# RMS norm cut into chunks and spread over groups of matmuls, conditioning pieces moved into the first attention, convolution statistics in two banks

## The reference

```python
for l in range(DEPTH):                                   # 4 layers: attention, convolution, attention, convolution
    sh1, sc1, g1, sh2, sc2, g2 = adaln(cond, w_ada[l], b_ada[l])      # silu(cond) @ w + b, six vectors of 1024
    h = modulate(rms_norm(x, norm_g[l, 0]), sh1, sc1)    # x*rsqrt(mean(x*x)+eps)*g, then h*(1+scale)+shift
    if l % 2 == 0:  y = attention(h) @ w_o               # also returns k and v of the context tokens
    else:           y = conv_module(h)                   # below
    x = x + g1 * y
    h = modulate(rms_norm(x, norm_g[l, 1]), sh2, sc2)
    x = x + g2 * (square(relu(h @ w_up[l])) @ w_down[l])
y = rms_norm(x, final_g)

def conv_module(h, ...):
    a, g = split(h @ w_pw1, 2);  u = a * sigmoid(g)
    u = depthwise_conv(u, width 31) + b_dw
    return silu(layer_norm(u, ln_g, ln_b)) @ w_pw2
```

## Time and profile before

| | us |
|---|---|
| median of three runs (lowest, highest) | 3113.19 (3110.22, 3113.33) |
| profiled execution | 3116.69 |
| its span on the slowest core (core 0) | 3115.1 |
| spans of the eight cores | 3084.0 to 3115.1 |
| TensorE, VectorE, ScalarE, GpSimd busy | 2656.1, 1152.1, 1135.2, 303.5 |
| 16 DMA engines, mean traffic | 65 GB/s |

### The profile page before, as it was taken

The page is one execution under the profiler, slowest core; times in us unless marked ns, Lnnn a source line. Parts: engine busy times, 40 slices in busy tenths (PEclk is TensorE's granted clock), DMA queues, the critical chain, the costliest instruction groups (busy, mean ns, idle before and its releaser), DMA issues.

```text
span 3115.1 us, 45413 instructions; the slowest of 8 cores (3084.0 to 3115.1 us)
## 1 busy us (share of the span) xinstructions
PE 2656.1 (85%) x15672; PEld 1154.0 (37%) x15672; DVE 1152.1 (37%) x1707; ACT 1135.2 (36%) x1800; POOL 303.5 (10%) x280
## 2 busy tenths in 40 slices
PE   1976878899997866999989778789999787699995
PEld 0432222344443432444434222234444343244442
DVE  0224453442323435423233444334232334542323
ACT  2424556530305245402153455654020523550214
POOL 0100000000002431000000000000000233200000
PEclk9985555999998998999999655589999898799997
DMA  8774110166652211466436411015665131033322
GB/s 175 122 181 61 8 8 1 28 90 100 102 93 44 56 26 17 79 100 101 78 57 162 90 12 8 1 28 82 95 95 82 29 75 26 1 54 55 54 42 81
DMA packets 107599, 202.28 MB, mean 65 GB/s; under 512 B 41904, under 2 KB 52144, under 8 KB 107376
## 3 DMA queue, kind: packets, MB, share of 16 engines
q0 software_dynamic: 76592, 154.23, 33.1%
q1 hardware_dynamic: 30784, 45.14, 4.4%
HBM read 315.02 MB, written 31.46 MB: 111 GB/s over the span
## 4 chain that ended last, share of the span: by engine, by line
PE 70%; ACT 13%; issue 7%; DVE 5%; DMA 3%; another core or an unknown queue 1%; ACTq 0%; DVEq 0%; SPq 0%
PE ps L612 45%; PE ps L1246 5%; ACT hTs L576 4%; PE ps L1211 3%; PE ps L857 3%; ACT scr L943 2%; PE ps L818 2%; PE ps L1376 2%; PE ps L860 2%; PE ps L636 2%; ACT scr L890 2%; DVE scr L936 1%; PE ps L909 1%; DMA vo<-scr 1%; PE ps L464 1%
## 5 line engine op out<-in xcount | busy, mean ns | idle before, releaser
L612 PE MATMUL ps<-hTs,ring 128*128 128x512 bf16 x3840 | 846.4, 382 | 39.3 <-ACT hTs L576 36.0
L612 PE MATMUL ps<-big,ring 128*128 128x512 bf16 x3072 | 666.7, 379 | 0.0
L612 PEld LDWEIGHTS ps<-hTs,ring 128*128 128x128 bf16 x3840 | 375.4, 98 | 497.4 <-issue 58.7
L677 ACT ACTIVATE big<-ps 128x512 f32<-128x512 f32 x384 | 227.2, 597 | 749.5 <-PE ps L612 741.6
L612 PEld LDWEIGHTS ps<-big,ring 128*128 128x128 bf16 x3072 | 299.2, 98 | 358.5
L679 DVE TENSOR_TENSOR big<-big 128x512 bf16<-128x512 f32 x384 | 265.1, 692 | 388.0 <-ACT big L677 385.5
L654 DVE SCALAR_TENSOR_TENSOR xTs<-ps,mod,xTs 128x512 f32<-128x512 f32 x240 | 178.5, 750 | 532.1 <-PE ps L612 500.6
L396 POOL DMA_DIRECT2D ring<-wall x140 | 100.2, 716 | 2080.7 <-PE ps L612 1385.6
L936 DVE TENSOR_TENSOR scr<-ps,scr 128x512 f32<-128x512 f32 (+7 forms) x384 | 189.9, 531 | 185.6 <-PE ps L922 146.2
L530 ACT ACTIVATE scr<-xTs 128x4096 bf16<-128x4096 f32 x27 | 97.6, 3616 | 435.1 <-DVE xTs L654 354.0
L943 ACT ACTIVATE scr<-scr 128x512 bf16<-128x512 f32 (+7 forms) x384 | 177.0, 503 | 184.6 <-DVE scr L936 152.5
(11 more groups left out here) (88 smaller groups left out, 1957.5 us busy)
## 6 DMA issues: line engine op xcount, KB each, us to landing
ring<-wall POOLq DMA_DIRECT2D x140, 1024.0 KB, 11.2
kTo<-scr SPq DMA_DIRECT2D x48, 256.0 KB, 6.7
vo<-scr SPq DMA_DIRECT2D x48, 256.0 KB, 3.2
scr<-big SPq DMA_DIRECT2D x128, 54.0 KB, 3.4
xTs<-xT SPq DMA_DIRECT2D x3, 2048.0 KB, 53.0
...
```

The costliest lines, as they stand in the source:

```text
L612: ins = e.matmul(ps[pi][:, :], lhsT=w[:, kc, fc * fw:(fc + 1) * fw], rhs=src[:, kc, t * 512:(t + 1) * 512], start=(kc == 0), stop=(kc == n ...
L677: P.op("act", lambda e: e.activation(out=ta[:, :], in_=ps[pi][:, :], func=AF.Relu), reads=[ps_r[pi]], writes=[ta_r])
```

## The change

**Norm.** `norm_begin` now comes before the stage that produces `xT`, and holds three PSUM banks, one per tile, out of `next_ps` (`held`). Behind each residual addition `norm_chunk` squares that one chunk (512 columns) on ScalarE and defers, with a lag of 1, a single sum matmul into the tile's bank. With the eighth the tile's Ln and Exp are issued and its eight outputs (`norm_out`) go on a second list, `bq`. `tick(rate)` first serves `pend`, then takes `rate` entries from `bq`: one as a rule, three in the "down" product. `ensure_h(t)` empties the lists as far as a product needs tile t. `hT_r` is one resource per tile and chunk. This holds for the output products, the second half of "down" in all layers (with the final norm) and "pw2".

**Conditioning.** The first four pieces run ahead of the first norm, the other eight of layer 0 one after each pair of heads in attention. The second and third tile of `xT` are loaded only when the third weight piece has landed.

**Convolution.** The sums of all three tiles of a chunk are six matmuls with a 32-column matrix of ones, each into 32 partitions of one of two banks (6 and 7), so that six banks are free for the rest. Mean and reciprocal deviation are computed once for 96 partitions and spread to 128 by float32 matmuls with `sel`. All tap matrices are built by VectorE, eight during each of "pw1" pieces 1 to 3 and the last eight between chunks. "pw2" writes its input in token order, so that its residual addition needs no strided view, and tile 1's and 2's LayerNorm chunks stand on `bq`.

```diff
-            sem_x[t], writes=[xT_r[c][t] for c in range(8)])
+            sem_x[t], writes=[xT_r[c][t] for c in range(8)],
+            extra=[(ring_sem[2], 16)] if t > 0 else [])
...
     pend = []
-
-    def tick():
+    bq = []
+
+    def tick(rate=1):
         for it in pend:
             it[0] -= 1
         while pend and pend[0][0] <= 0:
             pend.pop(0)[1]()
+        for _ in range(rate):
+            if bq:
+                bq.pop(0)[1]()
...
+    def ensure_h(t):
+        while any(it[1] == t for it in ntiles):
+            if pend:
+                pend.pop(0)[1]()
+            else:
+                bq.pop(0)[1]()
...
+    def norm_chunk(ctx, c, t, lag=1):
+        bk = ctx["bk"][t]
+        sq, sq_r = ctx["sq"][ctx["q"] % 6]
+        ctx["q"] += 1
+        P.op("act", lambda e: e.activation(out=sq[:, :], in_=xT[:, c, t * 512:(t + 1) * 512],
                                            func=AF.Square),
-             reads=[xT_r[c][t] for c in range(8)], writes=[ctx["sqb_r"][t % 2]])
...
+        def part():
+            n = ctx["cnt"][t]
+            ctx["cnt"][t] += 1
+            P.op("pe", lambda e: e.matmul(ps[bk][:, :], lhsT=ones_b[:, :], rhs=sq[:, :],
+                                          start=(n == 0), stop=(n == 7)),
+                 reads=[sq_r, const_r], writes=[ps_r[bk]])
+            if n == 7:
+                norm_rstd(ctx, t)
+                for cc in range(8):
+                    bq.append((t, lambda cc=cc: norm_out(ctx, cc, t)))
+        defer(lag, part)
+
+    def norm_rstd(ctx, t):
+        bk = ctx["bk"][t]
+        rstd, rstd_r = ctx["rstd"][t % 2]
+        P.op("act", lambda e: e.activation(out=rstd[:, :], in_=ps[bk][:, :], func=AF.Ln,
                                            bias=V("epsr"), scale=1.0 / D),
-             reads=[ps_r[pi], vecs_r], writes=[rstd_r])
...
+        P.op("act", lambda e: e.activation(out=ps[bk][:, :], in_=rstd[:, :], func=AF.Exp, scale=-0.5),
+             reads=[rstd_r], writes=[ps_r[bk]])
+
+    def norm_out(ctx, c, t):
         tsl = slice(t * 512, (t + 1) * 512)
-        for c in range(8):
-            ta, ta_r = ctx["tmp"][ctx["n"] % 2]
-            P.op("dve", lambda e, c=c, ta=ta: e.tensor_tensor(
-                out=ta[:, :], in0=xT[:, c, tsl], in1=rps[:, :], op=ALU.mult),
-                reads=[xT_r[c][t], rps_r], writes=[ta_r])
...
                 for fc in range(fc_per_piece):
-                    pi = next_ps(0, pshi)
...
                     evac(j, fc, t, pi)
-                    tick()
-                if last_tile_done is not None and j == npieces - 1:
-                    last_tile_done(t)
+                    tick(rate)
...
+    def resid_evac(gate_chunk0, nctx=None, lag=1):
         def evac(j, fc, t, pi, per_piece=4):
             fch = j * per_piece + fc
             s = slot_of(t)
@@ -656,17 +660,20 @@
                 scalar=md[:, gate_chunk0 + fch, s:s + 1], in1=xT[:, fch, t * 512:(t + 1) * 512],
                 op0=ALU.mult, op1=ALU.add),
                 reads=[ps_r[pi], cur["mod_r"][(gate_chunk0 + fch) // 4]], writes=[xT_r[fch][t]])
+            if nctx is not None:
+                norm_chunk(nctx, fch, t, lag)
         return evac
 
...
-                      pshi=pshi, last_tile_done=ltd)
+                      rate=3)
...
-        pshi = 8
-        linear_fm("qk", l, 4, 8, hT, hT_r, qk_evac, hook=adaln_piece, pshi=pshi)
+        linear_fm("qk", l, 4, 8, hT, hT_r, qk_evac)
...
             sched.append(("swap", None))
+            sched.append(("ada", None))
...
+            elif kind == "ada":
+                st["in_attn"] = True
+                adaln_piece()
+                st["in_attn"] = False
...
             w, w_r = wt[g % NWT]
-            P.op("dve" if g % 4 == 3 else "pool", lambda e: e.tensor_tensor(
+            P.op("dve", lambda e: e.tensor_tensor(
...
+        def stats(ch):
+            for half, bk in ((0, SMB), (1, SQB)):
+                src = sqc[:, half * 1536:(half + 1) * 1536].rearrange("p (f t) -> p f t", f=4)
+
+                def fn(e, src=src, bk=bk):
+                    ins = None
+                    for t in range(NT):
+                        ins = e.matmul(ps[bk][32 * t:32 * t + 32, :],
+                                       lhsT=ones_b[:, 0:32], rhs=src[:, :, t * 128:(t + 1) * 128],
+                                       start=(ch == 0), stop=(ch == 7), skip_group_check=True)
+                    return ins
+                P.op("pe", fn, reads=sq_r[half] + [const_r], writes=[ps_r[bk]])
 
...
                 P.op("pe", fn, reads=[w_[1] for w_ in ws] + src_r[::-1], writes=[ps_r[pi]])
+                if f == 0 and lag:
+                    stats(lag.pop(0))
...
                 conv_chunk(2 * j - 2)
+                if j == 3:
+                    for _ in range(4):
+                        build_w()
                 conv_chunk(2 * j - 1)
+        for _ in range(4):
+            build_w()
         conv_chunk(6)
         conv_chunk(7)
-        stats(*lag.pop(0))
+        stats(lag.pop(0))
...
+        def ln_bcast(t):
+            pm, pq = LB[t]
+            for pb_, src, src_r in ((pm, mean, mean_r), (pq, rstd, rstd_r)):
+                P.op("pe", lambda e, pb_=pb_, src=src: e.matmul(
+                    ps[pb_][:, :], lhsT=sel[32 * t:32 * t + 32, :], rhs=src[32 * t:32 * t + 32, :],
+                    start=True, stop=True),
+                    reads=[src_r, const_r], writes=[ps_r[pb_]])
...
+        gate = resid_evac(16, nctx)
+        ln_bcast(0)
+        for ch in range(8):
+            ln_chunk(0, ch)
+        ln_bcast(1)
+        for ch in range(8):
+            bq.append((-1, lambda ch=ch: ln_chunk(1, ch)))
...
+        held.add(3)
+        for t in range(NT):
+            while any(it[0] == -1 for it in bq) and t == 2:
+                bq.pop(0)[1]()
+            for fch in range(4 if t == 0 else 0, 8):
+                pi = next_ps()
                 pw2_mm(t, fch, pi, 0, 8)
-                conv_resid(fch, t, pi)
+                gate(0, fch, t, pi)
                 tick()
-            tdone(t)
-        st["pshi"] = 8
+            if t == 0:
+                while any(it[0] == -1 for it in bq) and len(bq) > 9:
+                    bq.pop(0)[1]()
+        held.difference_update((4, 5))
         for j in range(2):
...
-    rp0 = []
     adaln_begin(0)
+    for _ in range(4):
+        adaln_piece()
     for t in range(NT):
-        adaln_piece()
-        norm_A(ctx0, t)
-        rp0.append(norm_B1(ctx0, t))
-    adaln_piece()
-    for t in range(NT):
-        norm_B2(ctx0, t, *rp0[t])
+        for c in range(8):
+            norm_chunk(ctx0, c, t)
+            tick(0)
+    while pend:
+        tick(0)
```

393 lines of the change are left out of this document (162 added, 231 removed).

## The result

The changed kernel takes 3372.24, 3373.05 and 3375.03 us, against 3113.19 before: a ratio of 1.084 (95% interval 1.082 to 1.086). In some executions of these kernels the cores of one die run at a lower clock and the time is longer (3673.85 and 3739.96 for the changed kernel), and such executions are left out of all times in this document. The forecast was 3380. The profiled execution took 3372.24 with a span of 3370.7, against 3116.69 and 3115.1. The sum of the forecast came out almost exactly, but not from the terms that it was made of, as this part shows.

A forecast was written before the change was run, and what follows sets the result against it. It took TensorE's idle time, mainly at stage changes, as the bound. Gains of 87, 64 and 42 (193 us) against 285 of stalls gave 3205 at full clock; 175 for clock falls made 3380, range 3200 to 3510.

The forecast's parts named there:

- The stall, 285: Output product and second half of "down": 144 groups wait behind their own sum of squares, 285 us lost, bounds 202 and 346.
- The 1.98 us: Predicted TensorE wait per stalled group: residual addition, square on ScalarE and the signals between, from group's end to sum.
- The stage changes, 87: Changes of stage and tail: TensorE idle time around normalisation goes as outputs are spread, 87 us gained, bounds 70 and 97.
- the terms 42, 12 and 23: Stage-change gains: into the convolution 42 us, layer 1's MLP to layer 2's attention 12, the tail 23.
- 20 gained: Output product to the end of the first "up" piece: 10 us of lost time saved, twice.
- The convolution, 64: Both convolution layers: waits for tap matrices go as VectorE builds all ahead, 32 us a layer, 64 gained, bounds 40 and 71.
- The front, 42: Start to attention: moving conditioning pieces out of the front gains 42 us, bounds 20 and 55.
- I estimate 74: Start of the first product: estimated at 74 in place of 80.64, bounds 66 and 84.
- the 43: First product to first attention product: 43 us gained as six conditioning pieces, 2 MB of reads each, leave these stretches.
- The second pointwise product, 0: Pointwise product stage: 20 stalled groups a layer offset by other waits lost, no change, bounds 10 either way for both layers.
- The clock, 175: Stalled groups: every second of 184 gaps followed by a fall of TensorE's clock, 1.9 us each, 175 us lost.
- rival A: The stalls are there but TensorE's clock holds, giving 3205 us; chance 0.16.

The follow-up runs named there:

- e1: Changed kernel with each chunk's sum of squares put off by two ticks in place of one, in all stages; 3063.5 us, 0.983 of the kernel before.
- e7: e3 with three of four tap matrices built by GpSimd, at the new places in the order; 3061.9 us, 0.982 of the kernel before.
- e6: e3 with layer 0's conditioning pieces back behind the q/k and value pieces, none in attention; 3071.6 us, 0.985 of the kernel before.
- e10: e8 with only the first tile's input-norm sum ahead of the first product, the other tiles' squares behind its groups; 3026.6 us, 0.972 of the kernel before.
- e3: e1 with each normalised output's ScalarE half issued one tick behind its VectorE half; 3045.6 us, 0.977 of the kernel before.
- e8: e3 with the second pointwise product's Silu written contiguously and the residual addition reordering instead; 3036.7 us, 0.974 of the kernel before.
- e9: Changed kernel with each square of the second half of "down" done three times over on ScalarE; 3676 us, 1.180 of the kernel before.

## Why the prediction was right, and where it was not

The direction and its cause were right. "The chunk's callback is put off by one tick, but the tick comes at the end of the same group" decides the sign, and e1 shows it: with two ticks the same change is a gain.

**The stall, 285.** Measured by the distance between sums: 96 x 2.00 + 48 x 1.89 = 283; added up over all 144 groups of the trace it is 287, and 14 more for slower matmuls. The 1.98 us, put together from pieces of the earlier trace rows, were right to 0.1.

The next three terms were priced over stretches with other ends than those of the table: into the convolution up to the second tile's first product, the convolution from there to its last sum, the pointwise product from that sum to the end of the first "up" piece. So the table's figures are first moved to the prediction's own stretches.

**The stage changes, 87.** This step failed by 35. "Second half of down to next stage" cost 144.5, of which 192 are stalls: 47.5 gained. Up to the second tile's first product (18.4 us behind the first one before, 6.9 after, in each of two layers) it is 23 more, so 70.5 where the terms 42, 12 and 23 made 77: these were nearly right. The tail, for one, is 16.2 us, as estimated. "Output product and first up half" cost 108.2, of which 90 are stalls: 18 lost, where I had 20 gained. Here the path was wrong: of these 38, 20 are the wait ahead of the third tile (9.95 in both layers), about 10 are slower matmuls and about 6 stalls longer than 1.89. In sum some 52 in place of 87. I had kept back 10 us for outputs that "share ScalarE with the next stage's evacuations"; I counted the busy time of each engine and not that two in-order engines, each waiting for the other twice a round, run at the sum of their durations (0.69 + 0.68 + 0.81 + 0.57 us, 2.78 with the signals) and not at the longer one.

**The convolution, 64.** The table's 51 holds the 23 us just named and, against them, the chain ahead of the pointwise product, which grew by 10. By the prediction's stretch it is 38, below my lower bound of 40. The tap waits went, as said: 48.9 us before, none after. Of the 26 that are missing 15 are waits of 7.5 us ahead of the third tile in both layers; for outputs of that kind I had kept back 10 us over nine stage changes. That GpSimd builds nothing is worth 16 of the gain (e7), and that the builds stand earlier took the waits away.

**The front, 42.** 10 measured (29.2 less 5.6 less 13.6), below my lower bound of 20. Moving the pieces is worth 26 (e6). Two steps failed. "I estimate 74" for the start came to 86.25: with all sums ahead of the first product it waits for the last tile of x. e10 lets the first tile go ahead, worth some 8. I had named that order and not priced it. And the 43 for the way to the first value product came to 29.2, because in the first q/k piece TensorE waits 4.36 and 4.46 us ahead of the second and third tile and runs slow (9.78 and 9.54 us for 32 matmuls, 7.07 at full clock). Attention came out 13.6 dearer, not 10.

**The second pointwise product, 0.** It cost 55.5, 7.4 more in the "up" half behind it and 10 in the chain ahead of it: 73 in the prediction's stretch, outside its bounds of 10, and the largest miss beside the clock. I had let 80 us of stalls be paid for by other waits that go. They did not go: without the stalls (e3) the product itself is only 11.5 us shorter than before in two layers, and the "up" half behind it 19.8 longer. By layer 1, where 163.4 us stand against the 125.3 of the sum: 12.2 from the last sum to the first product (I had 10), 11.9 for the first groups with their chain (11.1), 104.7 for the twenty stalled groups with the burst (83.5), 34.4 for the "up" piece (20.7), in which TensorE waits for the third tile. The burst that I had put at "about 5" shows in the timeline, and so does that wait:

```profile
1255.74 9.05 ACT L1355 ACTIVATE hTs<-big,vecs_s 128x512 bf16<-128x512 f32 x7 [1.27 <-DVE big L1352]
...
1265.46 0.58 PE L560 MATMUL ps<-scr,onesb 128*128 128x512 bf16 x1 [8.06 <-ACT scr L553]
...
1354.20 8.98 PE L620 MATMUL ps<-hTs,ring 128*128 128x512 bf16 x32 [11.57 <-ACT hTs L597]
```

Seven Silu outputs of the third tile stand ahead of one square on ScalarE, and TensorE stands behind its sum for 8.06 us. Their stride I had not priced (e8: 1.50 us against 0.81).

**The clock, 175.** This step failed too: at most 22 by e1's busy time, and 9 by the distances between matmuls (59 against 50 before). In "down", where most of the stalls are, the clock stayed at 1.00 but for 3 of 96 groups, and I had written that I would be wrong in that case. From one gap of 1.96 us with a fall and one of 2.18 without I made "every second one". The gap of 1.96 ahead of 1186.93 in the earlier trace rows had another history:

```profile
1175.12 9.85 PE L1376 MATMUL ps<-hTs,ring 128*128 128x512 bf16 x32 [9.79 <-DVE xTs L1362]
```

TensorE had stood for 9.79 us shortly before it, and the 32 matmuls between ran in part at the lower clock (9.85 us in place of 7.07). A stall behind 3.5 us of dense matmuls at full clock, in a regular series of them, is not the same case; which of the two differences counts no run shows. Longer gaps at the same place do bring the fall (e9).

So 3205 at full clock, my rival A, was 167 us short, and this is what made it up: 32 in front, 35 at the stage changes, 73 in the second pointwise product, 26 in the convolution (what the clock cost lies within these). The clock term of 175 stood by chance in place of them. The range and the sign were earned, the 3380 was not.

Left open: how the 21 us that the twenty groups of a pointwise product cost above the sum divide between burst, stride and slower matmuls, and why the clock falls there (0.59 at 1240 to 1260) and is at 1.00 further on in the same product (1280 to 1300), with gaps of 1.7 to 1.8 us between groups of eight in both. The slow part holds waits of 3.09, 3.07 and 8.06 us besides; that they are the reason is not shown.
